# Two joints of a two-block layer kernel: when gating weights are split next to activated rows, and when two quarters of the last projection's weights are split inside the merge

## The reference, cut to what matters

```
z = jax.nn.gelu(s5_ssm(u, ...))            # 1024 x 512
z = z * jax.nn.sigmoid(z @ w_glu[l])       # "gl": the gating weights, 512 x 512
y_ssm = z @ w_ssm_branch[l]
...
y_a = (...) @ w_pa                         # "ap", 512 x 1024
y_b = (...) @ w_pb                         # "bp"
y_c = (...) @ w_pc                         # "cp"
merged = (jax.nn.sigmoid(g_a) * y_a + jax.nn.sigmoid(g_b) * y_b
          + jax.nn.sigmoid(g_c) * y_c)
return x + merged @ w_o                    # "w3", the last projection, 1024 x 1024
```

## Time and profile before

| what | value |
|---|---|
| median of three runs | 2056.04 us |
| the profiled execution | 2056.77 us |
| its span in the trace | 2055.0 us |
| TensorE busy | 2034.0 us, 99% |
| VectorE busy | 1268.2 us, 62% |
| ScalarE busy | 818.0 us, 40% |
| GpSimd busy | 280.2 us, 14% |

### The profile page before, as it was taken

How to read it: one execution, slowest core, us unless ns; L and a number is a source line. 1 busy time by engine, 2 the same in 40 slices (tenths; PEclk the granted TensorE clock), 3 DMA queues, 4 the chain that set the end, 5 groups by cost and what they waited for, 6 DMA issues and landing times.

```text
span 2055.0 us, 24239 instructions
## 1 busy us (share of the span) xinstructions
PE 2034.0 (99%) x9518; PEld 1686.0 (82%) x9518; DVE 1268.2 (62%) x1396; ACT 818.0 (40%) x1169; POOL 280.2 (14%) x507
## 2 busy tenths in 40 slices
PE   7999999999999999999999999999999999999998
PEld 6888888888888888888888888888888888888887
DVE  5337686848459777655566775674675756545552
ACT  5246666254224444323434543133444333432221
POOL 2576196000110000000000320200000000000200
PEclk9999999999999999999999999999999999999999
DMA  5633323577312544568656734022222111364513
GB/s 152 133 88 123 123 94 102 164 273 250 130 72 92 170 137 145 169 228 328 227 199 224 251 114 139 1 88 94 91 103 103 62 62 42 122 229 171 174 63 111
DMA packets 201301, 290.00 MB, mean 141 GB/s; under 512 B 27587, under 2 KB 130660, under 8 KB 200932
## 3 DMA queue, kind: packets, MB, share of 16 engines
q1 hardware_dynamic: 189264, 264.47, 38.5%
q10 hardware_dynamic: 11924, 23.98, 3.5%
HBM read 210.17 MB, written 77.07 MB: 140 GB/s over the span
## 4 chain that ended last, share of the span: by engine, by line
PE 94%; DVE 3%; ACT 1%; SPq 1%; DMA 1%; issue 1%; POOL 0%; POOLq 0%; ACTq 0%; DVEq 0%
PE A L2510 8%; PE A L2512 8%; PE A L2511 8%; PE X L2849 6%; PE X L2850 6%; PE X L2851 6%; PE A L2849 5%; PE A L2851 5%; PE A L2850 5%; PE X L2886 3%; PE X L2883 3%; PE X L2885 3%; PE A L2775 2%; PE A L2777 2%; PE A L2776 2%; PE A L2886 2%
## 5 line engine op out<-in xcount | busy, mean ns | idle before, releaser
L1673 DVE TENSOR_TENSOR WL<-raw,WH 128x1024 fp32r<-128x1024 f32 (+1 forms) x102 | 110.0, 1079 | 173.5 <-ACT WH L1081 173.3
L1081 ACT ACTIVATE WH<-raw 128x1024 fp32r<-128x1024 f32 (+1 forms) x102 | 88.7, 871 | 265.5 <-PE A L2512 165.9
L1687 DVE TENSOR_TENSOR WL<-S,WH 128x512 fp32r<-128x512 f32 x144 | 99.3, 690 | 99.8 <-ACT WH L1106 98.1
L2510 PE MATMUL A<-XH,WH 128*128 128x512 f32 x384 | 152.1, 396 | 0.6 <-DVE WL L1673 0.5
L2511 PE MATMUL A<-XL,WH 128*128 128x512 f32 x384 | 149.8, 390 | 0.0
L2512 PE MATMUL A<-XH,WL 128*128 128x512 f32 x384 | 149.6, 390 | 0.0
L1106 ACT ACTIVATE WH<-S 128x512 fp32r<-128x512 f32 x144 | 90.4, 628 | 134.0 <-PE X L2851 63.5
L1687 DVE TENSOR_TENSOR WL<-raw,WH 128x512 fp32r<-128x512 f32 x108 | 74.3, 688 | 93.6 <-ACT WH L1106 93.5
L2850 PE MATMUL X<-TL,WH 128*128 128x512 f32 x312 | 121.4, 389 | 0.0
L2849 PE MATMUL X<-TH,WH 128*128 128x512 f32 x312 | 121.4, 389 | 0.0
L2851 PE MATMUL X<-TH,WL 128*128 128x512 f32 x312 | 121.4, 389 | 0.0
(11 more groups left out here) (579 smaller groups left out, 5463.1 us busy)
## 6 DMA issues: line engine op xcount, KB each, us to landing
raw<-in_w_in SPq DMA_DIRECT2D x49, 1024.0 KB, 5.3
ring<-a_scr SPq DMA_DIRECT2D x26, 1024.0 KB, 9.0
ring<-in_w_ff_out SPq DMA_DIRECT2D x26, 1024.0 KB, 7.5
raw<-in_w_ff_in SPq DMA_DIRECT2D x16, 1024.0 KB, 7.9
a_scr<-SB SPq DMA_DIRECT2D x16, 1024.0 KB, 6.3
g_scr<-stage SPq DMA_DIRECT2D x24, 512.0 KB, 3.6
g_scr<-gst ACTq DMA_DIRECT2D x32, 256.0 KB, 3.1
x_scr<-xr ACTq DMA_DIRECT2D x16, 512.0 KB, 2.6
```

The source lines that it names most:

```text
L1081: A(unit_home(WH[:, r % 2, 0:kb, :], key), unit_of(raw[:, SLOT[p], 0:kb, :], key, i), ACT.Copy).then_inc(w_hi, 1)
L1673: TT(unit_home(WL[:, r, 0:kb, :], key), unit_of(raw[:, SLOT[p], 0:kb, :], key, i), unit_home(WH[:, r, 0:kb, :], key).bitcast(f32), ALU.sub ...
L1687: TT(seven_home(WL, p, j), seven_weights(p, j), seven_home(WH, p, j).bitcast(f32), ALU.subtract).then_inc(w_lo, 1)
L2510: mm(dst, WH[:, r, k, :], xh, start=(k == 0), stop=False)
```

## The change

The first edit swaps two calls in ScalarE's list: gelu(2) goes ahead of the high part of gating piece 1. The second moves the quarters 0 and 1 of the last projection's weights from the steps 4 and 5 of branch a to the steps 2 and 3, and the quarters 2 and 3 from 6 and 7 to 5 and 6, on ScalarE and on VectorE and in the common order. The order on each of them becomes: piece 4, quarter 0, piece 5, quarter 1, piece 6, piece 7, quarter 2, quarter 3 (before: pieces 4, 5, 6, quarter 0, piece 7, quarters 1, 2, 3). No transfer and no instruction is added or removed.

```diff
+W3_AT = (2, 3, 5, 6)
...
 for _i in range(4):
     _order.remove(("w3", _i))
-    _order.insert(_order.index(("ap", min(6 + _i, 7))) + 1 + max(0, _i - 1), ("w3", _i))
+    _order.insert(_order.index(("ap", W3_AT[_i] + 2 if _i < 3 else 7)) + 1 + (_i == 3), ("w3", _i))
...
             hi(("gl", 0))
+            gelu(2)
             hi(("gl", 1))
-            gelu(2)
             gelu(3)
...
                     if r < len(RING_KEYS):
                         hi(RING_KEYS[r])
-                    if s == "a" and f >= 4:
-                        hi(("w3", f - 4))
+                    if s == "a" and f in W3_AT:
+                        hi(("w3", W3_AT.index(f)))
...
                     merge(s, f)
-                    if s == "a" and f >= 4:
-                        lo(("w3", f - 4))
+                    if s == "a" and f in W3_AT:
+                        lo(("w3", W3_AT.index(f)))
```

## The result

The changed kernel takes 2059.43 us (median of 19 runs, 2057.43 to 2061.70), the kernel before 2055.78 us beside it (19 runs). The ratio is 1.0017, with a 95% interval of 1.0011 to 1.0023: between 2.3 and 4.7 us slower, where 3.0 us were forecast. The profiled execution of the changed kernel took 2060.07 us, its span 2058.3 us where before it was 2055.0 us. The changed file has one line more above the edits, so L2510 before is L2511 after, L1673 is L1674, and so on.

The account below looks back on a forecast made before the run. TensorE, busy 2034.0 of 2055.0 us, was taken as the bound. The merge's 3.1 us loss minus the gating stage's 0.1 us gain gave 3.0 us, so 2056.04 + 3.0 = 2059.0 us; range 2055.2 to 2060.9.

Parts of the forecast that it names:

- the ceiling: Removing TensorE's waits at the gating and merge edits can win at most 2.15 us, 0.1% of the time.
- Both old waits: TensorE's waits for gating row group 3, 1.46 us, and at branch a's tile 7, 0.69 us; both forecast to go.
- The first joint: Gating stage, gelu(2) ahead of piece 1's split: new 1.35 us wait at tile 1, old wait gone, 0.1 us gained.
- Rival 2: Gating stage: row group 2 lands 5.0 us after issue, costing 1.5 us there; total 2060.6 us; chance 0.12.
- The second joint: Branch a's merge: quarter splits and GpSimd additions serialise, tiles 5 and 6 late, tile 7 starts 3.1 us later.
- Rival 1: Merge: GpSimd's additions do not hold the quarters up; kernel 0.3 us faster, 2055.7 us; chance 0.15.
- the sum: Dating of branch a's steps 2 to 4 in the merge, with weight landings as profiled; tile 7 3.1 us later.

Follow-up runs that it names:

- quarters_only: Only the second edit (quarters at steps 2, 3, 5 and 6), gating order as in the kernel before: 2058.67 us beside 2056.03 us, ratio 1.0014.
- quarters_vector_adds: quarters_only with GpSimd's four additions of branch a made by VectorE, each ahead of its low part: 2056.43 us, ratio 1.0004 to the kernel before.
- quarters_panels_first: quarters_only with the raw weights of pieces 4 to 7 loaded ahead of the quarters: 2055.32 us beside 2056.18 us for the kernel before, ratio 0.9996.
- gate_weight_on_vector: The kernel before with the high part of gating piece 1 made by VectorE instead of ScalarE: 2054.89 us beside 2056.13 us, ratio 0.9993.
- gelu_only_third: The kernel before with only the first edit, gelu(2) ahead of gating piece 1's split, profiled a third time: 2055.91 us, one run.
- quarter0_early: The kernel before with quarter 0 at step 2 and quarters 1, 2, 3 at steps 5, 6, 7, gating order unchanged: 2057.98 us, ratio 1.0010.

## Why the prediction was right

**The bound and the ceiling.** Right: the page, then TensorE's waits, then the dates of its needs. Both old waits went, as forecast.

**The first joint, -0.1 us.** The mechanism holds where ScalarE is in time: gelu(2) starts when its load lands, the wait moves from `ZL` to the start of tile 1, and the swap gives no time that a measurement shows (1.0001, good to some 2 us). The delay of tile 1, forecast at 1.35 us, was 1.35 and 0.72 us in the two profiles that could show it. That the first agrees to the digit is luck: the load took 4.1 us and not 3.3, and TensorE came to the stage later by nearly as much, in part because of the stores. What the forecast did not see is that in seven of the thirteen profiles TensorE waits earlier, ahead of gating tile 0, because ScalarE was held issuing its stores. The one profile of before gave no hint of it. Rival 2 needed a landing 5.0 us after issue; where gelu(2) waited for it, it started 4.1 and 3.3 us after issue (438.12 - 434.03 and 435.56 - 432.26).

**The second joint, +3.1 us.** Right in place, kind and size. Forecast and measured, with quarters_only as the undisturbed case: `NL` 2.6 against 2.65 us, quarter 0 2.3 against 2.28, quarter 1 4.4 against 4.45, TensorE at tile 5 1946.6 against 1946.61, at tile 6 1953.9 against 1953.84, tile 7 without a wait, last projection 3.1 us later. In the changed kernel's own profile TensorE came to the merge 1.2 us late (`NH` of rows 0 at 1930.26 against 1929.10) while the weights landed only 0.3 us later (piece 4 split at 1937.88 against 1937.62). So its wait at tile 5 was 0.95 us, and the merge added 2.1 us there: 1.2 and 2.1 make the 3.3 us between the two spans.

**What is luck in the total.** The forecast adds 3.1 and -0.1 us. In the changed kernel's profile it was 2.1 us in the merge and 1.2 us ahead of it. Of the latter 0.2 us were there from the first 25 us of the kernel on, and most of the rest came in the gating stage and just ahead of it (the matmul of 445.87 before stands at 447.31 after), with the late stores. The two departures nearly cancel, and they belong together: tile 5 is bound by weights that land almost when they did, so a TensorE that comes late waits less there. The second edit alone measured 2.6 us by the medians, the two together 3.65 us; the intervals overlap, and whether late stores make up the difference isn't shown.

**The resolution.** The forecast put a change within 4.1 us, 0.2%, as one that a measurement can't tell from none. With 19 runs of each kernel the interval is 0.06% to either side, and the slowdown is clear of it.

**The rule on shared ports.** The Trainium skill, "SBUF — State Buffer", "Who interferes with whom": a VectorE instruction with two SBUF inputs and a GpSimd instruction that reads SBUF exclude each other, the second waits for all of the first. The trace agrees: 4.45 us beside an addition (`quarters_only`), 2.29 us with none (`quarters_vector_adds`), and the two stretched instructions of the changed kernel end 1.1 and 2.15 us after the addition beside them, nearly their whole unhindered lengths of 1.22 and 2.28 us. Rival 1, that they overlap, is refuted by that pair.

**What the prediction left out.** It charged the exclusion alone. quarters_panels_first shows that with the same exclusion and earlier weights nothing is lost, so the late landing of pieces 4 and 6, which the sum took as given, is needed for the greater part of the loss as much as the exclusion is.

## What to carry to other kernels

A split that moves to an earlier step pays there for what runs beside it. Before moving VectorE work with two SBUF operands, look for GpSimd instructions in the target steps and add the rest of each to it. And when a step starts late because of a transfer, mend the order of the transfers first: here the same placement made TensorE 3.1 us late behind late weights and 0.2 us behind timely ones.

## What was not expected of the hardware

Eight small stores issued by ScalarE, the same in every kernel, kept it for 4.55 to 7.44 us over thirteen profiles, and with the longest of them TensorE waits 1.9 us at the gating stage instead of 1.3. After the change the work reached the merge 1.2 us later, and the weights of piece 4 landed 0.3 us later; in gate_weight_on_vector, however, they landed 1.0 us earlier with work that was 0.6 us earlier, and in gelu_only_third 0.8 us earlier with work that was 1.8 us earlier. What decides how far a queued transfer moves with the work stays open.

In the merge of the profile of quarters_only TensorE's clock fell once. Of the windows of all engines, the ones around tile 5 (length, then busy time of PE, PEld, DVE, ACT, POOL, then granted clock, DMA share and GB/s):

```profile
1944.00:1946.50 2.50, 0.78 (x4) 0.32 (x2) 2.50 (x3) 0.25 (x1) 0.00 (x0) 1.00 0.74 258
1946.50:1947.80 1.30, 1.19 (x5) 1.05 (x6) 1.30 (x2) 0.31 (x1) 0.12 (x1) 1.00 0.07 23
1947.80:1951.00 3.20, 3.20 (x9) 2.52 (x8) 3.20 (x2) 0.34 (x2) 3.15 (x1) 0.50 0.00 0
```

After the wait of 1.82 us the granted clock was 0.50, the lower of its two levels (1.2 GHz), for some 3.2 us, and matmuls started 0.43 us apart instead of 0.23. It cost nothing here, since tile 6 had to wait for its piece until 1953.84 either way. The wait of 1.77 us in quarter0_early had no such fall.
